# Eight of twelve gate chunks per layer computed as seven half-size products, and the down weights' block sums moved behind the up products

## The reference, cut to what matters

```python
for l in range(DEPTH):                              # DEPTH = 2
    h = rmsnorm(x, norm_mix_pre[l])
    proj = jnp.einsum('bsd,de->bse', h, w_in[l])    # 512 x 1024 times 1024 x 5888
    qa, ka, va, pu, qc, kc, vc, gl = jnp.split(proj, splits, axis=-1)   # gl: 3 * 1024 columns
    ya = global_axial_attention(qa, ka, va, qk_norm_q[l], qk_norm_k[l])
    ...
    ys = jnp.stack([ya, yb, yc], axis=2)
    z = jnp.einsum('bsnc,ncd->bsnd', ys, w_branch[l])
    gates = jax.nn.sigmoid(gl + b_gate[l]).reshape(B, S, N_BRANCH, D_MODEL)
    merged = jnp.sum(gates * z, axis=2)             # over the 3 branches
    mix = jnp.einsum('bsd,de->bse', merged, w_out[l])
    x = x + rmsnorm(mix, norm_mix_post[l])
    h = rmsnorm(x, norm_ffn_pre[l])
    f = conv_gated_mlp(h, w_up[l], conv_w[l], conv_b[l], w_down[l])
    x = x + rmsnorm(f, norm_ffn_post[l])
```

## Time and profile before

| | |
|---|---|
| median of 3 runs | 3090.53 us (3089.28 to 3090.69) |
| the profiled execution's own time | 3087.93 us |
| its span, first to last instruction | 3086.1 us |
| granted TensorE clock, mean | 0.998 |
| TensorE busy | 3055.7 us, 99% of the span |
| VectorE busy | 1797.3 us, 58% |
| ScalarE busy | 1262.2 us, 41% |
| GpSimd busy | 173.3 us, 6% |

### The profile page before, as it was taken

One profiled execution on the slowest core, in us unless ns is written; L12 is line 12 of the kernel. 1 busy time (PEld: TensorE's weight loads), 2 busy tenths in 40 slices (PEclk: granted clock), 3 DMA queues, 4 the chain that ended last, 5 costly groups with the idle time before them and its releaser, 6 DMA issues.

```text
span 3086.1 us, 41574 instructions
## 1 busy us (share of the span) xinstructions
PE 3055.7 (99%) x16571; PEld 2508.3 (81%) x16571; DVE 1797.3 (58%) x2460; ACT 1262.2 (41%) x1788; POOL 173.3 (6%) x227
## 2 busy tenths in 40 slices
PE   8999999999999999999999999999999999999999
PEld 7767888888887688888888678888888888888887
DVE  3673446557755634655578866557743333465576
ACT  3563234335544622433365254336521221343355
POOL 2030000000021200000001100000000000000000
PEclk9999999999999999999999999999999999999999
DMA  6206853224542188232253147987423323332244
GB/s 181 66 28 224 193 143 110 95 95 143 167 93 79 60 252 194 96 109 95 95 191 110 56 170 198 298 192 219 150 91 109 110 82 110 103 109 95 95 136 157
DMA packets 298859, 408.96 MB, mean 133 GB/s; under 512 B 19925, under 2 KB 211453, under 8 KB 298461
## 3 DMA queue, kind: packets, MB, share of 16 engines
q1 hardware_dynamic: 251164, 306.75, 30.5%
q0 software_dynamic: 47552, 100.21, 13.7%
HBM read 400.54 MB, written 90.18 MB: 159 GB/s over the span
## 4 chain that ended last, share of the span: by engine, by line
PE 88%; DVE 8%; ACT 2%; DMA 2%; issue 1%; DVEq 0%; SPq 0%; ACTq 0%
PE ps L1980 20%; PE ps L1982 19%; PE ps L1981 19%; PE ps L2130 4%; PE ps L2131 4%; PE ps L2132 4%; PE ps L2082 2%; PE ps L2084 2%; PE ps L2083 2%; DMA t_wraw<-in_w_in_dram 2%; DVE t_wlo L1289 1%; PE ps L2191 1%; DVE t_vb L1809 1%; PE ps L2564 1%; PE ps L2562 1%; PE ps L2563 1%
## 5 line engine op out<-in xcount | busy, mean ns | idle before, releaser
L1980 PE MATMUL ps<-t_hh,t_whi 128*128 128x512 f32 (+1 forms) x2720 | 1014.9, 373 | 7.0 <-DVE t_hl L1376 4.2
L1982 PE MATMUL ps<-t_hh,t_wlo 128*128 128x512 f32 (+1 forms) x2720 | 1005.0, 369 | 0.0
L1981 PE MATMUL ps<-t_hl,t_whi 128*128 128x512 f32 (+1 forms) x2720 | 1005.0, 369 | 0.0
L1289 DVE TENSOR_TENSOR t_wlo<-t_wraw,t_whi 128x2048 fp32r<-128x2048 f32 x198 | 453.8, 2292 | 790.2 <-ACT t_whi L819 790.2
L819 ACT ACTIVATE t_whi<-t_wraw 128x2048 fp32r<-128x2048 f32 x198 | 379.4, 1916 | 1045.3 <-PE ps L1982 819.7
L1980 PEld LDWEIGHTS ps<-t_hh,t_whi 128*128 128x128 f32 x2720 | 513.3, 189 | 109.5 <-issue 21.1
L1981 PEld LDWEIGHTS ps<-t_hl,t_whi 128*128 128x128 f32 x2720 | 513.5, 189 | 86.8 <-issue 2.4
L1982 PEld LDWEIGHTS ps<-t_hh,t_wlo 128*128 128x128 f32 x2720 | 513.4, 189 | 86.9
L2130 PE MATMUL ps<-t_whi,t_ah 128*128 128x512 f32 x528 | 206.0, 390 | 0.0
L2132 PE MATMUL ps<-t_whi,t_al 128*128 128x512 f32 x528 | 205.5, 389 | 0.0
L2131 PE MATMUL ps<-t_wlo,t_ah 128*128 128x512 f32 x528 | 205.4, 389 | 0.0
(11 more groups left out here) (326 smaller groups left out, 4013.4 us busy)
## 6 DMA issues: line engine op xcount, KB each, us to landing
t_wraw<-in_w_in_dram SPq DMA_DIRECT2D x46, 1024.0 KB, 7.2
t_wraw<-in_w_up_dram SPq DMA_DIRECT2D x44, 1024.0 KB, 5.0
t_wraw<-in_ffn_w_in_dram SPq DMA_DIRECT2D x44, 1024.0 KB, 5.8
t_wraw<-sum_T SPq DMA_DIRECT2D x80, 512.0 KB, 4.2
sum_T<-in_w_down_dram POOLq DMA_DIRECT2D x12, 2560.0 KB, 31.8
sum_T<-in_ffn_w_out_dram POOLq DMA_DIRECT2D x12, 2560.0 KB, 30.9
sum_T<-sum_T POOLq DMA_DIRECT2D x8, 2560.0 KB, 20.3
t_wraw<-in_w_down_dram SPq DMA_DIRECT2D x34, 512.0 KB, 3.6
```

Source lines behind the costliest of these rows:

```text
L1289: v.tensor_tensor(wlo[slot][:, :], wraw[slot][:, :], whi[slot][:, :].bitcast(F32), ALU.subtract).then_inc(w_lo, 1)
L1980: te.matmul(out, wh, xh, start=first, stop=False)
L1981: te.matmul(out, wh, xl, start=False, stop=False)
L1982: return te.matmul(out, wl, xh, start=False, stop=last)
```

## The change

**Gate chunks.** In each of the two merges the chunks of branches 1 and 2 (four groups of two gate chunks and a branch chunk) are written out without a loop, and the eight gate chunks among them are computed by a seven-product scheme. A gate chunk's weights are cut into four blocks (two halves of the contraction, two output tiles: A11, A12, A21, A22), the tokens into two halves of 256. Instead of eight block products (two per quadrant of the result) there are seven, each of four contraction tiles times three, 12 matmuls of 128x256. Four of the seven take sums of weight blocks (s1 to s4), which GpSimd computes in `gain` (four instructions per chunk); four take combinations of `h` (`t1`, `t2`, `t4` in new buffers, and T3 written over one quadrant of `hh` and `hl`), which GpSimd, ACT and DVE prepare once per layer during the plain gate chunks. Four of the products' sums are copied aside from PSUM by ACT (`set_aside`: p1, p5, p4, u2), and DVE combines them with what stands in PSUM (`quarter_out`, four per chunk, in the place of two moves).

**Finer pieces.** The weights of these four groups are split in 18 pieces of 128 x 512 a group (seven per gate chunk, four per branch chunk) in a ring of eight slots laid over `whi` and `wlo`. A piece's slot is free when TensorE has used the piece eight places before.

**Down weights' sums.** `weight_sums(l)` stands behind `gains(2 * l + 1)`, so that its transfers run during the up products; `gains(2 * l)` waits for the last gate chunk, since `gain` is scratch until then.

The core of the diff. Slots and banks:

```diff
+    def op_free(l, o):
+        if o < 8:
+            return w_used, FIRST[f"merge{l}"] + PLAIN - 1 + o // 4
+        return op_used(l, o - 8)
...
+    def quadrants(q):
+        return [bank(4 * ((q + 1) % 2) + i)[:, 0:WIN] for i in range(4)]
+    p1, p5, p4, u2 = (gain[:, 2 * T + i * WIN:2 * T + (i + 1) * WIN] for i in range(4))
```

GpSimd:

```diff
                 pool.wait_ge(y_lo, PAIRS[f"A{l}"] + 4)
+                def difference(i, k1, t1, k0, t0):
+                    raw = raw_block(i)
+                    ch.link(gp.tensor_tensor(raw, h_block(hh, k1, t1).bitcast(F32), h_block(hh, k0, t0).bitcast(F32), ALU.subtract))
+                    ch.link(gp.tensor_tensor(raw, raw, h_block(hl, k1, t1).bitcast(F32), ALU.add))
+                    gp.tensor_tensor(raw, raw, h_block(hl, k0, t0).bitcast(F32), ALU.subtract).then_inc(t_sum, 1)
+                def rest_of(kh, th, done):
+                    raw = raw_block(2)
+                    pool.wait_ge(t_lo, 4 * l + done)
+                    ch.link(gp.tensor_tensor(raw, h_block(hh, kh, th).bitcast(F32), raw, ALU.subtract))
+                    gp.tensor_tensor(raw, raw, h_block(hl, kh, th).bitcast(F32), ALU.add).then_inc(t_sum, 1)
+                difference(2, 0, 1, 0, 0)
+                difference(3, 1, 1, 0, 1)
+                rest_of(1, 1, 1)
+                rest_of(1, 0, 2)
+                for i in range(2 * GROUPS):
...
+                    gp.tensor_tensor(s1, weight_block(cc, 1, 0), weight_block(cc, 1, 1), ALU.add).then_inc(g_sum, 1)
...
+                    gp.tensor_tensor(s2, s1, weight_block(cc, 0, 0), ALU.subtract).then_inc(g_sum, 1)
+                    pool.wait_ge(g_sum, n + 2)
+                    pool.wait_ge(*op_low(l, e + 1))
+                    gp.tensor_tensor(s1, weight_block(cc, 0, 1), s2, ALU.subtract).then_inc(g_sum, 1)
+                    pool.wait_ge(g_sum, n + 3)
+                    pool.wait_ge(*op_low(l, e + 4))
+                    gp.tensor_tensor(s2, weight_block(cc, 0, 0), weight_block(cc, 1, 0), ALU.subtract).then_inc(g_sum, 1)
+                pool.wait_ge(drained, 2 + DRAINS[f"merge{l}"] + 17)
                 gains(2 * l)
-                weight_sums(l)
                 pool.wait_ge(h_lo, SPLIT[f"pre{2 * l + 1}"] + 8)
                 gains(2 * l + 1)
+                weight_sums(l)
```

ACT:

```diff
+                for gi in range(GROUPS):
+                    n, g = divmod(gi + 2, 2)
                     for j in range(2):
+                        e = GROUP_OPS * gi + 7 * j
+                        xx, yy, _, ww = quadrants(3 * gi + PLAIN + j)
+                        set_aside(p1, xx, e)
+                        op_hi(op_next(e))
+                        set_aside(p5, yy, e + 1)
+                        for o in range(e + 1, e + 3):
+                            op_hi(op_next(o))
+                        set_aside(p4, ww, e + 3)
+                        op_hi(op_next(e + 3))
+                        set_aside(u2, xx, e + 4)
+                        for o in range(e + 4, e + 7):
+                            op_hi(op_next(o))
+                        if (gi, j) == (GROUPS - 1, 1):
+                            hi(c + 16)
+                        gate(n, g, j)
```

DVE:

```diff
+                        for o in range(e, e + 3):
+                            op_lo(op_next(o))
+                        dve.wait_ge(x_copied, i + 1)
+                        dve.wait_ge(*op_used(l, e + 2))
+                        quarter_out(n, g, j, 0, 0, zz, p1)
+                        for o in range(e + 3, e + 6):
+                            op_lo(op_next(o))
+                        dve.wait_ge(x_copied, i + 4)
+                        dve.wait_ge(*op_used(l, e + 5))
+                        quarter_out(n, g, j, 0, 1, yy, u2)
+                        dve.wait_ge(*op_used(l, e + 6))
+                        quarter_out(n, g, j, 1, 1, xx, p5)
+                        quarter_out(n, g, j, 1, 0, xx, p4).then_inc(drained, 1)
+                        op_lo(op_next(e + 6))
```

TensorE:

```diff
-                with pe.Fori(1, 3) as n:
-                    for g in range(2):
-                        for j in range(2):
-                            gate_rows(n, g, j)
-                        branch_rows(n, g)
+                def product(o, xh, xl, out, opens, l=l):
+                    wh, wl = op_slot(whi, l, o), op_slot(wlo, l, o)
+                    pe.wait_ge(*op_low(l, o))
+                    for k in range(4):
+                        kk = slice(k * P, (k + 1) * P)
+                        te.matmul(out, wh[:, kk], xh[:, k], start=opens and k == 0, stop=False, skip_group_check=True)
+                        te.matmul(out, wh[:, kk], xl[:, k], start=False, stop=False, skip_group_check=True)
+                        ins = te.matmul(out, wl[:, kk], xh[:, k], start=False, stop=k == 3, skip_group_check=True)
+                    ins.then_inc(op_used(l, o)[0], 1)
...
+                    product(e, *b11, xx, True)
+                    if e == 0:
+                        pe.wait_ge(t_lo, 4 * l + 4)
+                    product(e + 1, *t1, yy, True)
+                    product(e + 2, *b21, zz, True)
+                    product(e + 3, *t4, ww, True)
+                    pe.wait_ge(x_copied, i + 1)
+                    product(e + 4, *t2, xx, False)
+                    pe.wait_ge(x_copied, i + 2)
+                    product(e + 5, *b22, yy, False)
+                    pe.wait_ge(x_copied, i + 4)
+                    product(e + 6, *b12, xx, False)
```

More of the change, by code:

```diff
@@ L1155, in _, with op_hi @@
-                for g in range(2):
-                    for j in range(2):
-                        gate(2, g, j)
-                        if g == 1 and j == 0:
+                def op_hi(o, l=l):
+                    if o is None:
+                        return
+                    cc, gi, chunk, pos = op_place(l, o)
+                    act.wait_ge(*op_free(l, o))
+                    if chunk < 2 and pos in (1, 4, 5, 6):
+                        act.wait_ge(g_sum, 8 * GROUPS * l + 8 * gi + 4 * chunk + {1: 1, 4: 2, 5: 3, 6: 4}[pos])
+                    else:
+                        act.wait_ge(w_loaded[cc % 2], (cc // 2 + 1) * 16)
+                    sc.activation(by_k(op_slot(whi, l, o)), op_source(l, o), ACT.Copy).then_inc(op_high(l, o)[0], 1)
@@ L1161, in _ @@
                                 sc.activation(tile(yh, t), tile(mg, t), ACT.Copy).then_inc(h_hi, 1)
-                    if g == 0:
-                        hi(c + 14)
+                    for o in range(GROUP_OPS * gi + 14, GROUP_OPS * (gi + 1)):
+                        op_hi(op_next(o))
                 for t in range(4, KT):
```

171 lines of the change are left out of this document (147 added, 24 removed).

## The result

The changed kernel takes 3105.73 us (median of 7 runs, 3100.88 to 3116.64) beside 3089.55 us for the kernel before (7 runs, 3087.31 to 3090.69). The ratio is 1.0055, 95% interval 1.004 to 1.007: 16 us slower. The forecast was 3084.3, in a range of 3078 to 3096 us.

The account below looks back on a forecast made before the run. TensorE's own instruction stream was taken as the bound: -12.8 us for the shorter stream plus 6.6 us of new waits gives -6.2 us, from 3090.5 to 3084.3 us, in a range of 3078 to 3096 us.

Parts of the forecast that it names:

- What bounds the kernel; the stream: Merges: TensorE's own stream sets the time; a gate chunk falls from 10.88 to 10.08 us, sixteen chunks 12.8 us less.
- The moved transfers ... so cost 0: Start of the first two parts' up products: sums moved there meet the same loads as `ffn(3)`'s sums, cost 0.
- What the transfers cost in the old merges, taken as 0: Old merges: transfers leaving gives at most 1 us, since TensorE waits 1.1 us there in all; taken as 0.
- The second row: Profile rows cited for TensorE's waits in the two old merges: 0.8 us and 0.3 us.
- Waits in the merges, 6.6 us: Groups of seven-product gate chunks: TensorE's new waits at copies aside, 3.3 us a layer, 6.6 us for two layers.
- p1 first: First gate chunk of a merge: TensorE waits 0.9 us for ACT's copy p1, behind pieces waiting for GpSimd's s4.
- u2: Waits at the copy u2: 0.6 us in the second chunk, 0.3 us on each of two groups, per layer.
- p1 last: Last group of a merge: ACT's four copies of `mg` delay p1, 1.2 us with the restart.
- the steady state: Chunks after a branch: p1 of the next chunk is aside at 14.7 against a need at 15.84, 1.1 us of slack.
- Preparation, 0: Plain gate chunks: combinations of `h` ready at 290.9, wanted at 294.7, slack 3.8 us, so cost 0.
- GpSimd's sums come late: Rival, chance 0.15: DVE and GpSimd block each other in the merges, p1 misses by 2 us a chunk, +19 us, 3110 us.
- A little in each chunk: Rival, chance 0.2: each gate chunk waits 0.6 to 1.2 us at a copy aside, 10 to 19 us, 3088 to 3097.

Follow-up runs that it names:

- order_last: Changed kernel with ACT's first copies aside moved ahead, all sums' copies one after another, fourth part's sums at its own up products' start: 3077.82 us, ratio 0.9954.
- before_last: Kernel before with all sums' copies placed and issued one after another as in order_last, gate chunks untouched: 3089.7 us, ratio 0.9991.
- move_only: Kernel before with only the first two feed-forward parts' down-weight sums moved to where the changed kernel issues them: 3103.04 us, ratio 1.0035.
- move_late: Kernel before with the sums moved as in move_only, but started only when the third up chunk is split: 3095.52 us, ratio 1.001.
- move_serial: move_only with each of the four copies issued only when the one before it has landed: 3091.84 us, ratio 0.9999.
- gates_order: Changed kernel with sums started when the third up chunk is split, and ACT's first copies aside moved ahead in the merges: 3086.48 us, ratio 0.998.
- before_all: Kernel before, gate chunks untouched, sums of the two layers placed around their attentions, the third part's inside the convolution: 3097.33 us.
- order_serial: Changed kernel with copies one after another in all parts, and ACT's first copies aside moved ahead in the merges: 3087.27 us.
- order_all: Changed kernel with ACT's first copies aside moved ahead, layers' sums under their attentions, third part's sums inside the convolution: 3087.35 us, ratio 0.9973 to 0.9991.

## Why the prediction was wrong, step by step

**What bounds the kernel; the stream.** Right. 120 ns a matmul held, 10.08 us a chunk, -12.8 us; where most stops are gone the merges are 4.7 and 4.6 us shorter (order_last against before_last). That is 6.4 less the one stop left, 1.2 us with its restart, and some 0.55 us of stops too short to be listed.

**"The moved transfers ... so cost 0".** This step failed: they cost 11 us by move_only, 12.2 by the trace. It argued from the earlier trace rows, where the sums for `ffn(3)` run under up products in full swing. There each chunk has 10.88 us of work, and loads of up to 21 us found TensorE unbroken. It said "meet the same loads", but at the start of up products two chunks are consumed 5.8 us apart, and the first load, issued at 506.85 and wanted at 515.7, must land within 9 us. The median of 14.7 us in the earlier trace rows was far beyond that, and the load took 19.7. Keeping this one load clear of the copies (move_late) took away both long stops. The kernel before had a warning in its trace, which the forecast did not read: in `ffn(2)`, under its own sums, loads of 19.5 us issued from 1898 to 1912 and a stop of 0.92 us at 1926.

**The price of a stop.** Mostly missing from the working: after the long stops in `ffn(0)` and `ffn(1)` eight or more matmuls at the low clock, and some 0.25 us for the restart at each stop, which the forecast counted only in the last group.

**What the transfers cost in the old merges, taken as 0.** About right; their leaving gave 0.9 us in layer 0, nothing in layer 1. The second row lies behind layer 1's merge, whose own wait is one of 0.3 us for `t_gates`; the sum of 1.1 us stands by luck.

**Waits in the merges, 6.6 us.** The mechanism (copies aside late in ACT's queue) and the places p1 first, u2, p1 last were right, at 0.94, 0.5 to 1.5 and 1.58 us for 0.9, 0.3 to 0.6 and 1.2. The size was off: 13.1 us. The largest missing part is p1 of the second chunk, 1.4 us a layer, where ACT stands at the sigmoid, behind quarters that leave late in the first group:

```profile
323.76 1.06 ACT L1260 ACTIVATE t_gates<-t_gates 128x1024 f32<-128x1024 f32 x1 [1.42 <-DVE t_gates L1915]
324.73 0.37 ACT L1280 ACTIVATE t_gain<-ps 128x256 f32<-128x256 f32 x1
```

It was worked out for the steady state only (1.1 us of slack), and that was right there: no p1 stop in the two middle groups. Most of the rest is the restart, 0.25 us at each of seven stops.

**Preparation, 0.** Right in the result. The 1024-column instruction takes 2.4 us as estimated, three of the ten in a layer 3.3 to 4.5 us; TensorE did not wait.

**Rivals.** "GpSimd's sums come late" did not decide: with the sums made as before, ACT's order alone took the stops away. "A little in each chunk" gave the right size for the merges by another cause. No rival had the transfers. Without their 12.2 us the profiled 3106.15 would be 3094, inside the range.

**Left open.** The convolution's 1.6 us, and part of what `ffn(2)` lost: there a stop of 0.4 to 3 us comes behind late loads in nine of the ten kernels that issue its four copies together at its output products (0.92 us before, 2.04 after), and in none of the eight whose copies wait for each other. So it is the same fault, as far as this count shows; why its size differs between kernels with the same code there, the phase of the loads perhaps, was not shown.

## What to carry to other kernels

A transfer that is moved costs nothing only against the loads beside which it lands, at the place where it starts: list the loads one by one there, with the time each is wanted, and look at stage boundaries, where buffers are taken in quick succession; a median over a steady stretch says nothing of them. Bulk copies that nobody waits for belong one behind another, if their chain can be longer: here each chain grew by 15 us and TensorE got back 11 us, but where a second chain followed and was pushed under denser loads, some 6 us were lost again. In an in-order queue, put the short copy that frees the bottleneck engine ahead of whatever waits for a slower engine; that alone was worth 9 to 11 us in three pairs of runs, 9.2 in the traces of the merges.

## What the runs showed of the hardware that was not expected

- A load of 1024 KB on SP's queue takes 5.1 us with GpSimd's queue empty (before), 8.7 us beside one copy of 2560 KB (move_serial; 6.6 to 10.4 at that place in the other runs with copies one after another), 19.9 to 21.2 us beside four (after, move_only). A copy alone on its queue lands after 15.0 to 16.2 us; four issued together land after 17.5 to 44.
- After stops of 2.0 to 5.2 us TensorE ran seven to thirteen matmuls at 1.2 GHz, 0.43 us each, in eleven of the fifteen cases behind the kernel's start-up. It ran none slow after stops of 2.97 us in gates_order, 2.91 in before_all, 2.05 in order_serial and 2.01 in order_all, and none after stops up to 1.7 us.
- A stop of TensorE costs some 0.25 us beyond the listed wait: 0.16 us ahead of the first matmul, 0.10 in its slower start, at each of the stops of the merges.
